# Norm weights as a row ahead of the turns, H from PSUM, and the key and value blocks between the groups of cached index keys

## The reference

```python
h = rmsnorm(x, g_norm)                   # x * rsqrt(mean(x*x) + eps) * g
z = h @ w_in                             # 2048 -> 8720 columns, split as below
q_r, k_r, v_r, g_r, q_a, k_a, v_a, g_a, q_i, k_i, w_i = split(z)
# retention heads (8 of 128), chunkwise, with a state per head
# sparse attention: the indexer scores every key and keeps the best n_sel
rel   = relu(einsum('bqhd,bsd->bqhs', q_i, k_i_all))     # 16 index heads of 128
score = einsum('bqh,bqhs->bqs', w_i, rel)                # over cached + new keys
_, idx = top_k(score, n_sel)             # prompt: 128 of 512, sample: 256 of 4097
o_a = softmax(q_a . k_a[idx]) @ v_a[idx]                 # 8 heads, 2 key/value heads
x = x + concat(norm(o_r) * silu(g_r), o_a * silu(g_a)) @ w_out
y = rmsnorm(x, final_norm_g)
```

## Time and profile before

| | us |
|---|---|
| median of 3 runs (1239.47 to 1242.28) | 1240.18 |
| the profiled execution's own time | 1243.3 |
| its span, from the first to the last instruction | 1241.5 |
| TensorE busy in it | 1170.8 |
| VectorE busy | 637.2 |
| GpSimd busy | 577.5 |
| ScalarE busy | 452.3 |

### The profile page before, as it was taken

The page is one execution under the profiler, slowest core; times in us unless marked ns, Lnnn a source line. Parts: engine busy times, 40 slices in busy tenths (PEclk is TensorE's granted clock), DMA queues, the critical chain, the costliest instruction groups (busy, mean ns, idle before and its releaser), DMA issues.

```text
span 1241.5 us, 21876 instructions
## 1 busy us (share of the span) xinstructions
PE 1170.8 (94%) x9132; PEld 1109.9 (89%) x9132; DVE 637.2 (51%) x1201; ACT 452.3 (36%) x790; POOL 577.5 (47%) x267
## 2 busy tenths in 40 slices
PE   2899998988999999999999998999999998999995
PEld 2799997544999999999999998999999998999995
DVE  6700003898896997599998405254434537000013
ACT  5322323766223333333424232543434253323332
POOL 3525456042224222332536386848556474445450
PEclk9899998999999999999999999999999999999998
DMA  5423435185142321323343414454453424532313
GB/s 205 136 77 101 135 105 164 69 271 171 35 136 71 101 69 39 101 69 82 84 111 86 128 45 121 130 145 112 129 148 107 120 92 154 173 102 68 101 34 138
DMA packets 152838, 138.57 MB, mean 112 GB/s; under 512 B 4652, under 2 KB 145052, under 8 KB 151068
## 3 DMA queue, kind: packets, MB, share of 16 engines
q1 hardware_dynamic: 144500, 110.71, 29.9%
q0 software_dynamic: 6976, 22.03, 5.5%
q10 hardware_dynamic: 1280, 4.66, 1.0%
HBM read 127.01 MB, written 10.34 MB: 111 GB/s over the span
## 4 chain that ended last, share of the span: by engine, by line
PE 82%; DVE 10%; DMA 4%; issue 2%; ACT 1%; POOL 0%; DVEq 0%; ACTq 0%
PE bank L1451 24%; PE bank L1452 23%; PE bank L1453 23%; PE bank L1469 4%; DMA kx<-in_cache_kidx,pidx 3%; DVE bm L1088 2%; PE bank L1641 1%; PE bank L1659 1%; DVE cand L1154 1%; DVE top L1150 1%; DVE besti L1152 1%; DVE Hl L1051 1%; DMA XT<-in_x_prompt 1%; PE bank L1681 1%; DVE mix L1017 0%
## 5 line engine op out<-in xcount | busy, mean ns | idle before, releaser
L1451 PE MATMUL bank<-Hh,Wh 128*128 128x264 f32 (+2 forms) x2432 | 712.0, 293 | 2.1 <-DVE Hl L1288 0.8
L1452 PE MATMUL bank<-Hl,Wh 128*128 128x264 f32 (+2 forms) x2432 | 703.7, 289 | 0.6 <-issue 0.6
L1453 PE MATMUL bank<-Hh,Wl 128*128 128x264 f32 (+2 forms) x2432 | 702.4, 289 | 1.7 <-issue 1.6
L836 POOL TENSOR_TENSOR Wl<-Wraw,Wh 128x2048 fp32r<-128x2048 f32 x84 | 387.8, 4617 | 472.6 <-ACT Wh L484 472.2
L1451 PEld LDWEIGHTS bank<-Hh,Wh 128*128 128x128 f32 x2432 | 459.7, 189 | 6.7 <-issue 4.2
L1452 PEld LDWEIGHTS bank<-Hl,Wh 128*128 128x128 f32 x2432 | 459.7, 189 | 3.6 <-issue 3.3
L1453 PEld LDWEIGHTS bank<-Hh,Wl 128*128 128x128 f32 x2432 | 458.8, 189 | 2.8 <-issue 2.7
L484 ACT ACTIVATE Wh<-Wraw 128x2048 fp32r<-128x2048 f32 x84 | 160.4, 1911 | 365.9 <-PE bank L1453 365.7
L1391 DVE TENSOR_TENSOR Y<-Y,bank 128x512 f32 (+1 forms) x16 | 10.4, 685 | 159.2 <-PE bank L1469 159.2
L1072 DVE COPY QS<-mix 128x128 f32<-128x128 f32 x1 | 0.3, 281 | 146.1 <-ACT mix L490 146.1
L861 POOL DMA_INDIRECT kx<-in_cache_kidx,pidx x32 | 30.6, 955 | 55.8 <-PE bank L1469 48.8
(11 more groups left out here) (251 smaller groups left out, 1243.6 us busy)
## 6 DMA issues: line engine op xcount, KB each, us to landing
Wraw<-in_w_in SPq DMA_DIRECT2D x36, 1024.0 KB
Wraw<-in_w_in SPq DMA_DIRECT2D x64, 512.0 KB
Wraw<-in_w_out SPq DMA_DIRECT2D x16, 1024.0 KB
XT<-in_x_prompt ACTq DMA_DIRECT2D x4, 1024.0 KB, 8.7
sp__99<-in_state_ret SPq DMA_DIRECT2D x8, 512.0 KB, 4.2
out<-sp__99 SPq DMA_DIRECT2D x8, 512.0 KB, 5.0
Y<-in_x_prompt SPq DMA_DIRECT2D x1, 4096.0 KB
out<-Y SPq DMA_DIRECT2D x4, 1024.0 KB
```

Of the source, the lines that this page charges most:

```text
L836: nc.gpsimd.tensor_tensor(Wl[:, a, :, :], Wraw[:, a, :, :], Wh[:, a, :, :].bitcast(F32), ALU.subtract).then_inc(w_lo, 1)
L1451: mm(bank[i][:, 0:w], wh, Hh[:, kk, s], start=(a == 0 and k == 0), stop=False)
L1452: mm(bank[i][:, 0:w], wh, Hl[:, kk, s], start=False, stop=False)
L1453: last = mm(bank[i][:, 0:w], wl, Hh[:, kk, s], start=False, stop=(a == 1 and k == KC - 1))
```

## The change

Two things are changed together.

*At the start*, the norm weights are loaded once more as a row over all partitions (`gb`, 1 MB, ScalarE's DMA queue between blocks 1 and sample), and VectorE's scaling multiplies by factor and row in one operation. What TensorE turns is then H itself, and ScalarE and VectorE take Hh and Hl from PSUM: the gain products go, and so does GpSimd's part in Hl. GpSimd makes the low parts of the first chunk's weights, which move to the memory of mix. SyncE starts the first weights after the third arrival of the order in index (`x_in[2]`). TensorE does both halves of the index keys for tokens 0 to 255 in one go, and the last 264 tokens as 128 and 136.

*In the stage of the cached index keys*, chunks 9 and 10 no longer follow it: each of their eight banks of work (48 matmuls) is set behind a group given by the table BESIDE. They use banks 0 and 1; the sum over heads moves to bank 2. Their results go to the end of mix, and the keys are copied to kaT after the stage. GpSimd makes chunk 10's low parts behind gathers 21 and 23. TensorE waits for the scores before it turns keys and values.

```diff
+BESIDE = {1: (9, 0), 3: (9, 1), 5: (9, 2), 7: (9, 3), 9: (10, 0), 11: (10, 1), 13: (10, 2), 14: (10, 3)}
...
-            sp.wait_ge(x_in[1], 16)
+            sp.wait_ge(x_in[2], 16)
             weights(0, 0)
             weights(0, 1)
...
-            for i in ARRIVAL:
+            for pos, i in enumerate(ARRIVAL):
                 src = x_prompt[0, P * i:P * i + P, :] if i < QT else x_sample.rearrange("b o m -> (b o) m")
                 act.dma_start(XT[0:rows(i), i, :], src).then_inc(x_in[i], 16)
+                if pos == 1:
+                    act.dma_start(gb[:, :], norm_g[0].partition_broadcast(P)).then_inc(g_row, 16)
...
+            def keys_values_out(n, j):
+
+                t, half = j // 2, j % 2
+                act.wait_ge(acc_done, 4 * n + j + 1)
+                nc.scalar.activation((kaS if n == 9 else vaS)[:, t, part_tokens(half)], bank[j % 2][:, 0:part_width(half)],
+                                     ACT.Copy).then_inc(acc_free, 1)
...
                 relu_group(G)
                 if G < 15:
                     keys_out(4 * G + 7)
+                if G in BESIDE:
+                    n, j = BESIDE[G]
+                    if j == 3:
+                        hi(n + 1, 0)
+                    keys_values_out(n, j)
+                    if j == 3:
+                        hi(n + 1, 1)
...
-            for n in (9, 10):
-                hi(n + 1, 0)
-                if n == 9:
-                    act.wait_ge(sc_out, 3)
-                evacuate(n)
-                hi(n + 1, 1)
+            act.wait_ge(acc_free, 40)
+            nc.scalar.activation(kaT[:, :, :], kaS, ACT.Copy).then_inc(ka_home, 1)
...
-            for pos in range(4):
-                i = ARRIVAL[pos]
-                for g in range(4):
-                    v = 4 * pos + g
-                    pool.wait_ge(h_hi, v + 1)
-                    nc.gpsimd.tensor_tensor(Hl[:, 4 * g:4 * g + 4, tok(i)], raw_tile(v, rows(i)),
-                                            Hh[:, 4 * g:4 * g + 4, tok(i)].bitcast(F32), ALU.subtract).then_inc(h_lo, 1)
+            for a in range(2):
+                pool.wait_ge(w_hi, a + 1)
+                k = slice(KC * a, KC * a + KC)
+                nc.gpsimd.tensor_tensor(W0l[:, k, :], Wraw[:, a, :, 0:P], W0h[:, k, 0:P].bitcast(F32), ALU.subtract)
+                nc.gpsimd.tensor_tensor(W0h[:, k, P + NIH:P + 2 * NIH], Wraw[:, a, :, P:P + NIH],
+                                        W0h[:, k, P:P + NIH].bitcast(F32), ALU.subtract).then_inc(w_lo, 1)
+            pool.wait_ge(x_norm, 5)
             lo_loop(1, 10)
...
-                v_.tensor_scalar(XT[0:r, i, :], XT[0:r, i, :], st4[0:r, column(i):column(i) + 1], None,
-                                 ALU.mult).then_inc(x_norm, 1)
-
-            def gains(pos):
...
+                v_.scalar_tensor_tensor(XT[0:r, i, :], XT[0:r, i, :], st4[0:r, column(i):column(i) + 1], gb[0:r, :],
+                                        ALU.mult, ALU.mult).then_inc(x_norm, 1)
+
+            def low(pos):
+
+                i = ARRIVAL[pos]
                 for g in range(4):
                     v = 4 * pos + g
+                    dve.wait_ge(h_hi, v + 1)
+                    v_.tensor_tensor(Hl[:, 4 * g:4 * g + 4, tok(i)], turned_tile(v, rows(i)),
+                                     Hh[:, 4 * g:4 * g + 4, tok(i)].bitcast(F32), ALU.subtract).then_inc(h_lo, 1)
...
-                    else:
-                        v_.tensor_scalar(r, relu[:, i % 2, 0:w], wn[:, t, h:h + 1], None, ALU.mult).then_inc(si_acc, 1)
...
+            pe.wait_ge(h_lo, 8)
             pe.wait_ge(w_lo, 1)
-            pe.wait_ge(h_lo, 8)
-            index_keys(0, 0)
+            index_keys(0, slice(0, CUT))
+            pe.wait_ge(w_lo, 2)
+            index_keys(1, slice(0, CUT)).then_inc(acc_done, 1)
             turn_tokens(2)
+            index_weights(slice(P, CUT))
             turn_tokens(3)
             turn_tokens(4)
-            pe.wait_ge(w_lo, 2)
-            index_keys(1, 0).then_inc(acc_done, 1)
-            index_weights(slice(P, CUT))
             pe.wait_ge(h_lo, 16)
-            pe.wait_ge(h_lo_last, 4)
-            index_keys(0, 1)
-            index_keys(1, 1).then_inc(acc_done, 1)
+            for a in range(2):
+                index_keys(a, slice(CUT, CUT + P))
+            pe.wait_ge(h_lo, 20)
+            for a in range(2):
+                last = index_keys(a, slice(CUT + P, NT))
+            last.then_inc(acc_done, 1)
...
                 if G < 15:
                     turn_keys(4 * G + 7)
+                if G in BESIDE:
+                    keys_values(*BESIDE[G])
...
-            chunk(9, 0, lambda: pe.wait_ge(sc_out, 3), at_=1)
-            chunk(9, 1)
-            chunk(10, 0)
-            chunk(10, 1)
 
             pe.wait_ge(acc_free, 44)
+            pe.wait_ge(sc_out, 3)
```

More of the change, by code:

```diff
@@ L525, in evacuate @@
                     act.wait_ge(acc_done, 4 * n + place_ + 1)
-                    if n <= 10:
-                        ins = nc.scalar.activation((kaT if n == 9 else vaT)[:, t, s], src, ACT.Copy)
-                    elif n <= 18:
+                    if n <= 18:
                         j = (n - 11) // 2
@@ L863, in _ @@
                     bass.IndirectOffsetOnAxis(ap=pidx[:, b, s:s + 1], axis=0)).then_inc(kx_in[v % 6], 16)
-            lo_loop(10, 19)
+                if v == 21:
+                    lo(10, 0)
+                if v == 23:
+                    lo(10, 1)
+            lo_loop(11, 19)
             kr = cache_k[0].rearrange("n s c d -> (n s) (c d)")
@@ L1033, in _ @@
+            link(v_.tensor_copy(gains_T[:, :], bank[3][:, 0:KT + NH]))
             norms(0, 2)
+            dve.wait_ge(g_row, 16)
             scale(0)
             scale(1)
[L1036 to L1039, removed]
             norms(2, 5)
-            first_weights_low(0)
+            low(0)
+            low(1)
             scale(QT)
             scale(2)
-            first_weights_low(1)
@@ L1045, in _ @@
-            gains(2)
             scale(3)
[L1047 to L1052, removed]
+            low(2)
+            low(3)
+            low(4)
             dve.wait_ge(s_const, 80)
             dve.wait_ge(s_ptab, 16)
-            dve.wait_ge(h_lo, 16)
@@ L1058, in _ @@
-            dve.wait_ge(h_lo_last, 4)
+            dve.wait_ge(h_lo, 20)
+            link(v_.memset(bm[:, :], 0.0))
             link(v_.tensor_tensor(ptm[:, :, :], ptb[:, :, :].rearrange("p b (s j) -> p (b s) j", s=SEC),
@@ L1087, in _ @@
                         dve.wait_ge(si_acc, i)
-                        v_.scalar_tensor_tensor(r, relu[:, i % 2, 0:w], wn[:, t, h:h + 1], r, ALU.mult, ALU.add).then_inc(si_acc, 1)
-                    else:
-                        v_.tensor_scalar(r, relu[:, i % 2, 0:w], wn[:, t, h:h + 1], None, ALU.mult).then_inc(si_acc, 1)
+                    v_.scalar_tensor_tensor(r, relu[:, i % 2, 0:w], wn[:, t, h:h + 1], r, ALU.mult, ALU.add).then_inc(si_acc, 1)
                     i += 1
@@ L1489, in _, with index_keys @@
             turn_tokens(1)
-            def index_keys(a, half):
-                s, out = part_tokens(half), bank[half][:, 0:part_width(half)]
+            def index_keys(a, s):
+                half = s.start >= CUT
+                out = bank[half][:, s.start - CUT * half:s.stop - CUT * half]
                 for k in range(KC * a, KC * a + KC):
-                    mm(out, W0h[:, k, 0:P], Hh[:, k, s], start=(k == 0), stop=False)
-                    mm(out, W0h[:, k, 0:P], Hl[:, k, s], start=False, stop=False)
+                    wh = W0h[:, k, 0:P]
+                    mm(out, wh, Hh[:, k, s], start=(k == 0), stop=False)
+                    mm(out, wh, Hl[:, k, s], start=False, stop=False)
                     last = mm(out, W0l[:, k, :], Hh[:, k, s], start=False, stop=(k == KT - 1))
@@ L1585, in row_product, with keys_values @@
                 pe.wait_ge(wsel_ready, 1)
-                mm(bank[half][32 * half:32 * half + NS * SEC, :], wsel[:, g, NS * SEC * s:NS * SEC * s + NS * SEC],
+                mm(bank[2][32 * half:32 * half + NS * SEC, :], wsel[:, g, NS * SEC * s:NS * SEC * s + NS * SEC],
                    (wiT, relu2)[half][:, 0:T], start=(G < 2), stop=(G >= 14), tile_position=(0, 32 * half)).then_inc(sc_row, 1)
+            def keys_values(n, j):
+                t, half = j // 2, j % 2
+                s, out = part_tokens(half), bank[j % 2][:, 0:part_width(half)]
+                if n == 10 or j >= 2:
+                    pe.wait_ge(acc_free, 4 * n + j - 1)
+                for a in range(2):
+                    if j == 0:
+                        pe.wait_ge(w_lo, 2 * n + a + 1)
+                    for k in range(KC):
+                        kk = ktile(n, a, k)
+                        wh, wl = Wh[:, a, k, tile_cols(t)], Wl[:, a, k, tile_cols(t)]
+                        mm(out, wh, Hh[:, kk, s], start=(a == 0 and k == 0), stop=False)
+                        mm(out, wh, Hl[:, kk, s], start=False, stop=False)
```

(5 more changed lines are left out.)

60 lines of the change are left out of this document (25 added, 35 removed).

## The result

The changed kernel takes 1281.2 us (median of 4 runs, 1279.9 to 1285.5) against 1240.95 of the kernel before in the same series: a ratio of 1.033 (95% interval 1.0317 to 1.0344), or 40 us more. The forecast was 1266.6, at most 1275: right in sign and in its main step, 14.6 us short. The profiled execution is the slowest of the four (1285.5 us); its span is 1283.6 us, 42.1 more than before.

What follows compares the result with a forecast made beforehand. TensorE was taken as the bound, busy 1170.8 of 1241.5 us. A first-head resumption 23.9 us later, start and stage terms included, plus 2.5 of cold clock gave +26.4 on 1240.2: 1266.6 us, range 1255 to 1275.

Steps and rivals of the forecast that it cites:

- main step: At the first head's turns: TensorE waits 27 us for VectorE's probabilities and resumes 23.9 us later than before.
- What stood behind the scores: 45.5 us of matmuls moved ahead of the scores delay VectorE's selection; TensorE waits 27 us at the first head.
- Rival 1: Selection after the scores stays hidden, so the first head isn't held up: 1236.7 us; chance 0.04.
- The stage: Cached index keys: +3.5 us beyond the 45.5 of inserted matmuls, between 0 and +7.
- The regular waits: TensorE's repeated waits for gathers in the cached index keys' stage, claimed to stay at 5 us.
- The stall near the tenth group: In the stage, chunk 10's subtraction delays gathers 22 and 23: TensorE waits about 3.3 us more.
- the loop of release, gather and need: In the stage, pieces lie outside it: about 6.1 us of TensorE work against 6.7 of gather, so waits stay.
- Rival 2: In the stage, the pieces do hide the waits: -6.8 instead of +3.5, 1256 us; chance 0.08.
- The wait at the last relu: At the stage's end, ScalarE makes chunk 11's weights ahead of the last relu: +1.4 us.
- The start: Up to chunk 1, which begins at 54 to 55 instead of 63.6: -9 us, between -10.5 and -3.
- Rival 3: The start gives little, by 128-column matmuls at 0.139 us or a late gain row: -3, 1273 us; chance 0.10.
- First operation of the index scores: VectorE's scaling there becomes a three-input one: taken as 0, bound -3.8 us.

Runs made afterwards that it cites:

- sel34: Changed kernel with 34 instead of 56 selection steps ahead of the first head's logits, and chunk 17's weights issued earlier: 1260.2 us, ratio 1.0157.
- before_sel76: Kernel before with 76 instead of 56 selection steps ahead of the first head's logits, no matmul moved: 1253.4 us, ratio 1.0099.
- nosplit: Changed kernel with the last 264 tokens of the index keys in one matmul each, not 128 and 136: 1278.5 us, ratio 1.0297.
- even: Changed kernel with the eight pieces of chunks 9 and 10 behind groups 0, 2, ..., 14 instead of 1, 3, ..., 13, 14: 1266.9 us, ratio 1.0205.
- start_only: Only the start's change on the kernel before, blocks 9 and 10 left behind the scores: 1242.1 us, ratio 1.001.
- port: Changed kernel with VectorE's last three scalings waiting for GpSimd's low parts of the first weights: 1272.0 us, ratio 1.024.

## Why the forecast was right in kind and too small

- *What stood behind the scores: right.* First maximum to first turns took 447.3 - 368.9 = 78.4 us, forecast 79.9; the wait was 25.0, forecast 27, and behind it the granted clock was 0.50 from 447 to 452 us, as forecast. That it is the queue order and not the moved matmuls as such is shown from both sides: sel34 takes the wait away with the matmuls still moved, before_sel76 makes one without moving any. Rival 1 is refuted: the slack is there and covers what is below 16 us.
- *The stage: right in mechanism, mis-sized.* "+3.5 us beyond the 45.5, between 0 and +7" was 10.6. Three terms were too small. The regular waits did not stay at 5 us but summed to 8.9; in nosplit, with the same stage, they summed to 6.3, so part of this changes from execution to execution, and its cause stays open. The stall near the tenth group was 5.7 us where 3.3 more were forecast: the gather was issued late by those 3.3 us, and it then took 6.39 us to land, where the forecast reckoned with 5.17. And the half clock behind these waits (3 to 4 us) had no term at all, though the earlier trace rows told of it at the start. The wait at the last relu was 0.9 us, forecast 1.4. That the piece lies outside the loop of release, gather and need is shown by even: one group earlier and all gather waits go. Rival 2 would have been nearly right for pieces in that place: the stage of even is 4.4 us shorter than 66.4 + 45.5, where rival 2 had 6.8. By the fit in the Trainium skill, DMA: Bandwidth & Descriptors, Anatomy of one DMA — SWDGE (gpsimd) path, such a gather would take 3.2 us, an estimate; on the chain of the changed kernel they take 4.9 to 6.4. The prediction's "+1.4" for the stage by that figure doesn't follow from its own terms: +3.5 less the 5.1 us of regular waits is -1.6.
- *The start: the step that failed.* "-9 us, between -10.5 and -3" was 0 (-0.3 at chunk 1, start_only 1.001). Two terms were wrong, the first by 5.5 us, the second by 4. The forecast had GpSimd's low parts "ready at 25.8 and 29.6" at "half of 4.62 us plus some 0.4 each"; the first was ready at 25.0, the second only at 36.8. I had used and the earlier trace rows to say that VectorE is held for a whole GpSimd instruction, and never asked what happens when VectorE comes first: then GpSimd is held. The Trainium skill, SBUF — State Buffer, Who interferes with whom, says that a VectorE instruction with two SBUF inputs contends with a GpSimd instruction that reads SBUF, and that the order of issue decides who blocks. The trace agrees (8.57 against 2.36 us, and 2.38 in port). And the 96 short matmuls were taken at 0.07 us, the lower of the bounds 0.07 and 0.139; they took 0.112, 4 us more. Rival 3 named the short matmuls, not the held GpSimd; only both together take the whole 9. The Trainium skill, TensorE: Matmul & The Clock Gate, Back-to-back issue gap, has 0.081 us for such pairs and the trace 0.112: nearer than my value, still too low.
- *First operation of the index scores: right*, at 0. TensorE waits 3.9 us for that relu, as before.
- *Later heads: right.* No second stall came, and nothing was given back.

The sum closes: 1266.6, +9 for the start, +7 for the stage, -2 for the shorter wait, is 1280.6.

## What to carry to other kernels

Before moving work ahead of a long dependent series, read what the series gates in its own engine's queue, and take its slack from the profile: here 16 us, and 45 were put ahead of it. A piece that is to hide a transfer has to stand between the instruction that frees the buffer and the one that needs it; one group further on it hides nothing. When a subtraction of GpSimd is set beside an operation of VectorE that reads two tiles of SBUF, work out both orders of arrival: here whichever started first kept the other waiting.

## What the runs showed of the hardware

- A GpSimd subtraction of 128x1024 took 2.36 us beside VectorE operations that read PSUM, 8.57 behind three on 2048 columns with two SBUF inputs (6.86 us), and 2.38 with VectorE idle. In the kernel before it was VectorE's turn: 0.16 us steps took 1.2 beside GpSimd.
- Pairs of weight load and matmul at 128 to 136 float32r columns came every 0.112 us, at 264 columns every 0.12.
- In the stage the granted clock was 0.50 (1.2 GHz) from 283 to 286 us and from 314.7 to 320, each behind a wait of TensorE for a gather (2.19 and 5.7 us), and TensorE was busy 4.0 us longer than for the same 817 matmuls in even (106.44 against 102.46). With the pieces one group earlier and no gather wait left, the stage kept 1.00.
- In the changed kernel the first gather after a pause took from 4.3 us (issued at 339.23, awaited until 343.55) to 6.05 us (issued at 275.06) from issue to landing, with no subtraction of GpSimd beside it. The cause stays open.
